# Neighbourhood attention: the first heads' output projection moved between the steps of the last attention

## The reference, cut to what matters

```python
def c_mixer(u, uc, in_w, out_w, rpb, need_ctx):
    ...
    q, k, v, z = proj(u)
    ...
    o = neighbourhood_latent(q, k, v, k_c, v_c, rpb)   # (1, 512, 16 * 64)
    y = (o * jax.nn.silu(z)) @ out_w                   # out_w: 1024 x 1024
    ...

def neighbourhood_latent(q, k, v, kc, vc, rpb):
    ...
    s_loc = jnp.einsum('bqhd,bkhd->bhqk', qr, kr).astype(jnp.float32) * scale + bias.astype(jnp.float32)
    s_loc = jnp.where(mask, s_loc, -jnp.inf)
    s_ctx = jnp.einsum('bqhd,bkhd->bhqk', qr, kc).astype(jnp.float32) * scale
    p = jax.nn.softmax(jnp.concatenate([s_loc, s_ctx], axis=-1), axis=-1)
    ...

# around it, in the last layer
h = h + gate * y
return rms_norm_2(h, final_g)
```

## Time and profile before

| | us |
|---|---|
| median of 3 runs | 2908.92 (2906.0 to 2909.6) |
| the profiled execution, whole | 2904.34 |
| its span | 2902.5 |
| oc0, TensorE from first matmul to that of pc1 | 2647.90 to 2678.38 |
| pc1 | 2678.38 to 2776.83 |
| na1 | 2776.83 to 2861.75 |
| oc1 and the end | 2861.75 to 2902.5 |

### The profile page before, as it was taken

How to read it: one execution, slowest core, us unless ns; L and a number is a source line. 1 busy time by engine, 2 the same in 40 slices (tenths; PEclk the granted TensorE clock), 3 DMA queues, 4 the chain that set the end, 5 groups by cost and what they waited for, 6 DMA issues and landing times.

```text
span 2902.5 us, 35739 instructions
## 1 busy us (share of the span) xinstructions
PE 2723.8 (94%) x14462; PEld 1781.7 (61%) x14462; DVE 1175.4 (40%) x2636; ACT 652.3 (22%) x1372; POOL 287.5 (10%) x274
## 2 busy tenths in 40 slices
PE   8999999999999999999999999998899998999998
PEld 6878764554544576776753444443777667865864
DVE  5363443112122643424341111113664556665576
ACT  2130421123222100000021010001352442053053
POOL 2020001111110000001001111100200001112111
PEclk9999999999999999999999999999989999999999
DMA  5804059999999622132379999999100112220310
GB/s 185 326 4 174 30 232 382 417 414 412 378 419 373 245 78 82 64 130 99 127 306 407 420 419 419 414 414 418 62 30 32 68 39 84 77 80 33 96 26 37
DMA packets 118846, 613.33 MB, mean 211 GB/s; under 512 B 12813, under 2 KB 25165, under 8 KB 92944
## 3 DMA queue, kind: packets, MB, share of 16 engines
q1 hardware_dynamic: 96096, 546.17, 47.2%
q0 software_dynamic: 19904, 53.65, 5.5%
q10 hardware_dynamic: 2672, 11.09, 1.0%
HBM read 587.79 MB, written 38.80 MB: 216 GB/s over the span
## 4 chain that ended last, share of the span: by engine, by line
PE 75%; DMA 9%; DVE 6%; PEld 3%; ACT 3%; issue 2%; PEldq 0%; SPq 0%; ACTq 0%; DVEq 0%; POOLq 0%
PE psum L753 24%; PE psum L2346 12%; DMA ring<-in_expert_w_gu 8%; PE psum L2366 6%; PE psum L653 6%; PE psum L1029 5%; PE psum L889 5%; PE psum L1061 3%; PE psum L1049 3%; PE psum L643 2%; PE psum L1345 2%; PEld psum L753 2%; PE psum L2339 1%; DMA arena<-in_expert_w_gu 1%; PE psum L2352 1%
## 5 line engine op out<-in xcount | busy, mean ns | idle before, releaser
L2346 PE MATMUL psum<-ring,XT 128*64 128x512 f32 x1024 | 242.8, 617 | 28.7 <-DMA ring<-in_expert_w_gu 27.8
L2346 PE MATMUL psum<-arena,XT 128*64 128x512 f32 x1024 | 235.6, 605 | 7.0 <-DMA arena<-in_expert_w_gu 6.6
L2489 DVE TENSOR_TENSOR XT<-XT,psum 64x512 f32<-64x512 f32 x64 | 44.1, 690 | 488.3 <-ACT XT L2492 488.3
L753 PE MATMUL psum<-arena 128*128 128x256 f32 x1056 | 239.1, 380 | 2.8 <-DVE arena L740 2.8
L753 PEld LDWEIGHTS psum<-arena 128*128 128x128 f32 x1056 | 200.4, 190 | 31.4 <-DVE arena L740 4.0
L1029 PE MATMUL psum<-arena 64*128 64x384 f32 (+7 forms) x736 | 187.5, 473 | 25.8 <-ACT arena L1086 14.8
L753 PE MATMUL psum<-XT,ring 128*128 128x256 f32 x864 | 198.6, 385 | 7.1 <-ACT XT L474 3.1
L753 PEld LDWEIGHTS psum<-XT,ring 128*128 128x128 f32 x864 | 165.9, 193 | 34.5 <-issue 5.7
L2346 PEld LDWEIGHTS psum<-ring,XT 128*64 128x64 f32 x1024 | 75.3, 142 | 173.0 <-issue 130.9
L2346 PEld LDWEIGHTS psum<-arena,XT 128*64 128x64 f32 x1024 | 78.0, 139 | 141.9 <-issue 140.0
L1074 ACT ACTIVATE arena<-psum 128x512 f32<-128x512 f32 (+3 forms) x304 | 133.0, 477 | 123.0 <-PE psum L1049 121.5
(11 more groups left out here) (400 smaller groups left out, 3970.9 us busy)
## 6 DMA issues: line engine op xcount, KB each, us to landing
ring<-in_expert_w_gu SPq DMA_DIRECT2D x64, 2048.0 KB, 18.6
arena<-in_expert_w_gu SPq DMA_DIRECT2D x64, 2048.0 KB, 20.4
arena<-in_expert_w_down SPq DMA_DIRECT2D x32, 2048.0 KB, 13.6
ring<-in_expert_w_down SPq DMA_DIRECT2D x32, 2048.0 KB, 11.9
ring<-in_ada_w SPq DMA_DIRECT2D x12, 2048.0 KB, 9.0
ring<-in_fox_w_in SPq DMA_DIRECT2D x8, 2048.0 KB, 12.4
ring<-in_ret_w_in SPq DMA_DIRECT2D x8, 2048.0 KB, 10.6
ring<-in_c_in_w SPq DMA_DIRECT2D x8, 2048.0 KB, 7.7
```

Source lines behind the costliest of these rows:

```text
L753: m = pe.matmul(ps[0][:, 2 * P * i:2 * P * (i + 1)], x, w, start=(not onto and i == 0 and c == 0), stop=(c == 3), skip_group_check=True)
L2346: i = pe.matmul(psum[side * BR:(side + 1) * BR, 0:FF], x[:, 4 * part + c, :], w[:, c, side * FF:(side + 1) * FF], start=(part == 0 and c = ...
```

## The change

The stage oc0 is gone. Its work becomes the `inner` list of na1, called oc0 still, on bank 7 alone. The list has 35 entries: the diagonals on VectorE; two jobs that spread the gate, of 512 columns each, into banks 6 and 7, each with a copy by ScalarE; and 16 jobs (called M below) of four matmuls of 256 columns, each multiplied by the gate on VectorE, and a sum by GpSimd for each. The outputs of the pairs in na1 then have bank 6 alone (`a.OUT = 6,`), so a pair's first W waits for the multiplication of the pair before. The first W of all waits for the gate's copy out of bank 6. For g = 0 the gate `ZT` lies in `HC` (the context's residual, no longer read), as it must live until na1. ScalarE and GpSimd get the calls for the inner list, and GpSimd's loop goes by steps: tables loaded at step 8 and 16, windows added at step 10 and 18.

```diff
@@ class Attend
-            inner = None
+            inner = first_out = None
@@ Attend.weigh
                 pe.wait_ge(self.s("pt"), self.at("pt") + self.first[2 * m + 2])
+                if i == pair == 0 and self.first_out:
+                    self.inner.taken(pe, self.first_out)
                 if i == 0 and pair >= len(self.OUT):
                     pe.wait_ge(self.s("out"), self.at("out") + pair + 1 - len(self.OUT))
@@ Attend.act, after the exponential
+                    if self.inner and n:
+                        self.inner.drains(act, "a", *self.share(n - 1))
@@ Neighbours.pool
-                for pair in range(1, self.heads // 2 - 1):
-                    pool.wait_ge(self.s("max"), self.at("max") + 2 * NT * pair)
-                    for h in range(2 * pair + 2, 2 * pair + 4):
-                        self.load(pool, h)
-                    self.band(pool, range(2 * pair + 2, 2 * pair + 4))
+                for n in self.steps():
+                    pair = n // (2 * NT)
+                    if n % (2 * NT) == 0 and 1 <= pair < self.heads // 2 - 1:
+                        pool.wait_ge(self.s("max"), self.at("max") + 2 * NT * pair)
+                        for h in range(2 * pair + 2, 2 * pair + 4):
+                            self.load(pool, h)
+                    if n % (2 * NT) == 2 and 1 <= pair < self.heads // 2 - 1:
+                        self.band(pool, range(2 * pair + 2, 2 * pair + 4))
+                    if self.inner and n:
+                        self.inner.drains(pool, "p", *self.share(n - 1))
@@ mixer_c
-                u = Weights.add((0, 4, D, io["c_out_w_2"][0][512 * g:512 * (g + 1), :]))
-                if g:
-                    LastProj(f"oc{g}", u, 4, ZT, NT, 1).unit = u
-                else:
-                    use_units(OutProj(f"oc{g}", u, 4, ZT, NT, 1), u)
+                if not g:
+                    first_gate = ZT
+                    continue
+                us = [Weights.add((0, 4, D, io["c_out_w_2"][0][512 * k:512 * (k + 1), :])) for k in range(2)]
+                a.OUT = 6,
+                GATE, DIAG, TMP = region(18432, D), region(19456, KC, P), region(20480, 4, 256)
+                x = a.inner = Products("oc0", width=1, on=(7,)).inline()
+
+                def diagonals(dve, ps):
+                    for c in range(KC):
+                        i = dve.tensor_scalar(DIAG[:, c, :], ident, modc[:, 1, 16 + c, 0:1], None, ALU.mult)
+                    return i
+                laid = x.side("v", diagonals)
+                gate = []
+                for half in range(2):
+                    def fill(pe, ps, half=half):
+                        for c in range(4):
+                            i = pe.matmul(ps[0][:, c * P:(c + 1) * P], ones, DIAG[:, half * 4 + c, :], start=(c == 0), stop=(c == 3),
+                                          skip_group_check=True)
+                        return i
+                    gate.append(x.job("a", fill, act_out(GATE[:, BANK * half:BANK * (half + 1)], ACT.Copy), after=[laid], onto={"banks": [6 + half]}))
+                a.first_out = gate[0]
+                sums = []
+                for n in range(4 * NT):
+                    t, at = n // 4, slice(256 * (n % 4), 256 * (n % 4 + 1))
+                    made = x.job("v", mm_R(us[0], 0, 4, D, at.start, 256, first_gate, t),
+                                 lambda dve, ps, n=n, at=at: dve.tensor_tensor(TMP[:, n % 4, :], ps[0][:, 0:256], GATE[:, at], ALU.mult),
+                                 units=(us[0],), release=(1,) if n == 4 * NT - 1 else (), needs=[gate[n % 4 // 2], *sums[max(0, n - 4):max(0, n - 3)]])
+                    sums.append(x.side("p", lambda pool, ps, t=t, n=n, at=at: pool.tensor_tensor(H[:, t, at], TMP[:, n % 4, :], H[:, t, at], ALU.add),
+                                       needs=[made]))
+                use_units(x, us[0])
+                LastProj("oc1", us[1], 4, ZT, NT, 1).unit = us[1]
```

More of the change, by code:

```diff
@@ L1087, in act @@
                                        bias=sm[:, 0, n:n + 1], accum_out=sm[:, 1, n:n + 1]).then_inc(self.s("exp"), 1)
+                    if self.inner and n:
+                        self.inner.drains(act, "a", *self.share(n - 1))
+                if self.inner:
+                    self.inner.drains(act, "a", self.share(n)[0])
             def before_exp(self, act, n):
@@ L3389, in pool @@
             def pool(self, pool):
-                for pair in range(1, self.heads // 2 - 1):
-                    pool.wait_ge(self.s("max"), self.at("max") + 2 * NT * pair)
-                    for h in range(2 * pair + 2, 2 * pair + 4):
-                        self.load(pool, h)
-                    self.band(pool, range(2 * pair + 2, 2 * pair + 4))
+                for n in self.steps():
[8 more added lines that the diff above has]
+                        self.inner.drains(pool, "p", *self.share(n - 1))
+                if self.inner:
+                    self.inner.drains(pool, "p", self.share(n)[0])
             def band(self, pool, heads):
@@ L3417, in mixer_c @@
                 QT, KT = region(6144, 2, 4, SEQ), region(10240, 8, NTA // 2 * P)
-                V, ZT = region(13312, NTA, 512), region(16384, 4, SEQ)
+                V = region(13312, NTA, 512)
+                ZT = region(16384, 4, SEQ) if g else HC[:, :, :].rearrange("p (r a) n -> p r (a n)", r=1).rearrange("p r (c n) -> p (r c) n", c=4)
                 p = BandProducts(f"pc{g}")
```

## The result

| | before | with the change |
|---|---|---|
| median of 9 runs, us | 2906.0 (2902.4 to 2911.1) | 2915.25 (2912.8 to 2921.0) |
| ratio of the two, 95% interval | | 1.0034 (1.0024 to 1.0043) |
| profiled execution, us (span) | 2904.34 (2902.5) | 2918.24 (2916.4) |
| na1: first scores to first row of oc1 | 84.92 | 125.63 |
| oc0 | 30.48 | 0 |

The change makes the kernel 0.34% slower, 10 us (7 to 12.5 by the interval). The profiled execution shows where: na1 grew by 40.7 us, and 30.5 went with oc0, so 10.2 us are lost inside this pair of stages. The rest of the difference of the two spans, 3.7 us, lies ahead of na1 (it starts at 2750.01, and 2776.83 - 30.48 would be 2746.35). Almost all of it is there when na0 begins, 2566.61 against 2563.05, in stages that were not changed; na0, whose GpSimd loop did change, takes 84.94 against 84.85. The runs of one kernel differ by as much.

A forecast was written before the change was run, and what follows sets the result against it. TensorE was taken as the bound, busy 94% of the span. oc0 gone -30.5, sixteen M +27.7, gate jobs +1.8, start waits +3.9 and +2.3, clock 0, one bank +1.2, filled idle -2.2, end +0.4: +4.6 us, 2913.5 us, range 2909 to 2920.

The forecast's parts named there:

- three signs of being wrong: In na1: an M waiting for its bank in the steady part, clock at 0.50 beyond the first M, or first waits absent.
- The two waits: At na1's start TensorE waits for VectorE's diagonals, +3.9 us, and before the first M for ScalarE's gate copy, +2.3 us.
- The clock: At na1's start, some 1.5 us lost at the low clock again, as in the run before: net 0.
- The rival on the clock: After na1's start the clock stays low for 10 to 14 us of work: in all +8 to +10 us, chance 0.2.
- The M: Sixteen M on TensorE in na1 cost 1.73 us each, as read from one in fa1: +27.7 us.
- The check against oc0: oc0's 56 records of 512 columns and the gate's 16 took the same sum, so narrower matmuls gain or lose nothing.
- The one bank: In na1 a pair's first W waits 0.6 us for the output bank at two pair boundaries: +1.2 us, bounds 0 and 2.
- The filled idle time: M fill na1's gaps in two later exponential waits and among the last transposes and W: -2.2 us, bounds -2.5 and -1.4.
- The end: At na1's end the last M, VectorE and GpSimd's sum give 1.44 us idle instead of 0.99: +0.4 us, bounds 0 and 1.5.
- The M's wait for bank 7: In na1's steady part no M after the first was to wait for its bank; such a wait would show the forecast wrong.
- waits half as long: Rival: na1's start costs 3.3 us instead of 6.2, in all +1.7 us, 2910.6 us, no change; chance 0.18.
- M partly free: Rival: M stand in slack of na1's chain of scores, maximum and exponential; 0.65 of each hidden gives 2902 us; chance 0.06.

The follow-up runs named there:

- e1: The changed kernel with VectorE laying the eight diagonals before unit 0's maximum, not behind unit 1's normalisation: 2912.8 us, ratio 1.0021 to the kernel before.
- e8: The changed kernel with ScalarE copying each gate half in the step where TensorE makes it, not one later: 2910.25 us, ratio 1.0014 to before.
- e3: The changed kernel with filler matmuls on TensorE in na1, 14 behind unit 1's scores and 16 behind unit 2's: 2912.85 us, ratio 1.0019 to before.
- e4: The kernel before with 14 filler matmuls behind unit 1's scores in both neighbour attentions: 2903.89 us, ratio 0.9996 to before.
- e5: The kernel before with one output bank in both neighbour attentions and nothing else: 2908.83 us, ratio 1.0012 to before.
- e6: The changed kernel with gate jobs behind unit 1's scores, diagonals and earlier gate copy on ScalarE, M at steps 4 to 34: 2901.79 us, ratio 0.9985 to before.
- e2: The changed kernel with the 16 M at steps 4, 6, ..., 34, always behind transposes: 2911.33 us, ratio 1.0018 to before.
- e7: As e6, with the last projection taking na1's gate and spreading none of its own: 2897.01 us, ratio 0.9968 to the kernel before.

## Why the prediction was right, and where it was short

The direction and the range held: 2913.5 was forecast in 2909 to 2920, and the median is 2915.25. That the number came so near is in part luck. The likeliest sum, +4.6 us, is half of the measured 10; the forecast was counted from a median of 2908.92 for the kernel before, which nine runs put at 2906.0, and this 2.9 us made up for part of what the sum lacked. The prediction also held a time within 0.2% of before to be likelier (0.53) than a slower one (0.41), and the slower one came. Of its three signs of being wrong two came: an M waited for its bank, and the clock stayed at 0.50 beyond the first M, until 2775. Point by point:

- **The two waits** were right in place, cause and size: 3.86 for the diagonals and 2.27 for the copy. They come from reading each engine's order at the start and adding durations of rows along it. e1 and e8 took them away one at a time.
- **The clock** is the step that failed. It was booked at 0, one new low stretch against the 1.5 us of the one before. There were two low stretches and they cost 4.3 on work that sets the end (e3 gives 2.5 for the first; in e8 the second is gone with its wait). And e4 shows that the 1.5 of before was worth nothing. The rival on the clock named three idle times close together as the danger. The clock did not stay low in one piece for 10 to 14 us of work, as that rival has it; it came back and fell a second time, with some 8.6 us of work at the low level in all (twice 4.3, an estimate). Its sum, +8 to +10, is nearer to the measured 10 than the forecast's. Both times the clock came back while TensorE worked without a gap: from 2760.95, and the granted clock is 1.00 from 2765 to 2766; from 2770.32, and it is 0.99 from 2775 to 2776. The Trainium skill, "TensorE: Matmul & The Clock Gate", section "Part 1: The HAM clock gate", says that activity releases the throttle; both returns in na1 agree.
- **The M** cost 1.73 behind transposes as in fa1 and 1.92 behind W; the row of fa1 chosen for the price was one behind transposes (1.89 long), while fa1's M behind W read 1.99 to 2.00. A term mis-sized by 1.3. (The check against oc0 named the wrong rows: it is the 8 + 56 records of 512 columns, 3.5 + 24.2, that make 27.7, without the gate's 16.)
- **The one bank** was right: 0.53 at two boundaries and none at the third. The earlier trace rows left open who released W; the rows after and e5's name VectorE.
- **The filled idle time** was right, 2.3.
- **The end** was mis-sized: 1.25 instead of 0.4. GpSimd's sum took 0.72 and not 0.63, and after it 0.87 passed until the next stage began, where VectorE's drain in the kernel before was followed after 0.3. The price of a barrier behind GpSimd had no row before; the timeline after shows it:

```profile
2873.93 0.72 POOL L3500 TENSOR_TENSOR H<-arena,H 128x256 f32<-128x256 f32 x1 [2.66 <-DVE arena L3498]
...
2875.52 1.66 DVE L910 TENSOR_SCALAR arena<-cst,modc 128x128 f32<-128x128 f32 x8 [1.66 <-POOLq L3523]
```

- **The M's wait for bank 7**, 0.5 once, was named only as a way to be wrong. By the rows it comes from the window's sum on GpSimd, below.
- The rivals with waits half as long and with M partly free did not come true. The waits had their full length, and so had each M. TensorE has slack only in na1's first steps, as e4 and e6 show.

What stays open: why the first maximum of na1 begins 0.4 us later with the change (2751.53 for scores that start at 2750.01, against 2777.98 for 2776.83). The distance is 1.52 to 1.53 in e2, e3, e6, e7 and e8 too, and 1.15 in e4, e5 and in na0 of the changed kernel, so it goes with the inner list; by what, was not tried.

## What to carry to other kernels

Here work that was moved between the steps of a busy stage cost its full time on the engine that bounds the stage, so the gain is at most the barrier and the idle time it can fill; look for that idle time first and put the pieces with long preparation there. Read the in-order queue of each helper engine up to the point where it releases the moved work: in this stage's first steps the pipeline was empty, and a wait on a helper that was not yet through stopped everything behind it. Idle time on TensorE can cost twice, once as a wait and once as the low clock after it, but the second only where TensorE and not another chain sets the pace: e3 gained 2.5 us by holding the clock, na1 of e4 nothing.

## What the hardware showed that was not expected

A sum on GpSimd stretches VectorE's normalisation. After the change, ScalarE's and TensorE's rows are plain at 2789 to 2792, and VectorE's is not (0.62 is its usual time):

```profile
2789.26 4.44 POOL L3413 TENSOR_TENSOR arena<-arena,cst 128x896 f32<-128x896 f32 x2 [3.35 <-DMA arena<-in_bands]
...
2789.36 2.40 DVE L1141 TENSOR_SCALAR arena<-arena,rt 128x768 f32<-128x768 f32 x1
...
2791.68 0.41 DVE L3498 TENSOR_TENSOR arena<-psum,arena 128x256 f32<-128x256 f32 x1
...
2792.15 1.99 PE L653 MATMUL psum<-ring,HC 128*128 128x256 f32 x8 [0.49 <-DVE arena L3498]
```

The normalisation begins 0.1 us after GpSimd's first of two sums of 896 columns and ends 2.4 later, 0.3 after that sum (half of 4.44 is 2.22). In e5, where it begins 0.7 after the sum, it ends 0.3 after it too. The Trainium skill, "SBUF — State Buffer", section "SBUF: two separate sides", describes the port pair that VectorE and GpSimd share as an exclusive lock that blocks the other side for a whole instruction; on VectorE's side it names operations in a mode that uses two ports or with two operands in SBUF. These rows agree in length; no run here shows the mode or the lock itself. The take of the M is queued behind it on VectorE, and so the next M waited 0.49. The second window stretched the normalisation as much (2.46 at 2816.13), but no M waited there. This is no effect of the change: in the kernel before, the normalisation at 2802.83 took 2.13 beside such a sum, and the scores at 2807.41 then waited 0.63 for the exponential.

Matmuls of 256 columns take 1.92 for a job behind W, whose weights are 64 columns wide, and 1.73 behind transposes: 0.19 more, at each of seven places. Behind transposes and without a wait the M begins 0.71 after the transposes' start, and scores in its place 0.80 after; behind W nothing of the kind is seen. An M that has waited takes 1.92 behind transposes too (2792.15 to 2794.07). So the width of the weights may not be the reason; it was not tried apart.
